# The first norm of a two-block forward pass: rows of x scaled as they land, and a new order of the first weight tile

## The reference

```python
def rms_norm(x, g):
    xf = x.astype(jnp.float32)
    y = xf * lax.rsqrt(jnp.mean(xf * xf, axis=-1, keepdims=True) + NORM_EPS)
    return (y * g.astype(jnp.float32)).astype(x.dtype)

h = rms_norm(x, norm1_g[l])
proj = h @ w_in[l]
...
x = x + (g_a * y_attn + g_b * y_conv) @ w_out[l]
```

## Time and profile before

| | us |
|---|---|
| Median of three executions | 1408.19 (1407.58 to 1408.29) |
| The profiled execution, its own time | 1409.79 |
| Span of the profiled execution | 1407.9 |
| TensorE busy in the span | 1390.3 |
| VectorE, ScalarE, GpSimd busy | 763.4, 599.8, 600.4 |
| Mean granted clock of TensorE | 0.996 |

### The profile page before, as it was taken

The page is one execution under the profiler, slowest core; times in us unless marked ns, Lnnn a source line. Parts: engine busy times, 40 slices in busy tenths (PEclk is TensorE's granted clock), DMA queues, the critical chain, the costliest instruction groups (busy, mean ns, idle before and its releaser), DMA issues.

```text
span 1407.9 us, 20943 instructions
## 1 busy us (share of the span) xinstructions
PE 1390.3 (99%) x7688; PEld 1153.6 (82%) x7688; DVE 763.4 (54%) x1512; ACT 599.8 (43%) x1030; POOL 600.4 (43%) x318
## 2 busy tenths in 40 slices
PE   7999999999999999999999999999999999999998
PEld 6878777778898888888888978878898888888887
DVE  4797865555767665667784848532563232221221
ACT  5322555455345444443222524575354344342222
POOL 8442222115435444444553479623335444444441
PEclk9999999999999999999999999999999999999999
DMA  6941110114524444445763151021213222322321
GB/s 197 204 114 38 60 61 31 31 31 148 181 92 154 150 128 149 134 136 157 219 194 102 61 119 61 31 61 31 90 61 120 89 89 100 109 86 82 108 83 60
DMA packets 187269, 146.15 MB, mean 104 GB/s; under 512 B 21545, under 2 KB 185619, under 8 KB 187200
## 3 DMA queue, kind: packets, MB, share of 16 engines
q1 hardware_dynamic: 185488, 144.59, 34.0%
q10 hardware_dynamic: 1200, 0.36, 0.1%
q0 software_dynamic: 512, 0.25, 0.1%
HBM read 143.08 MB, written 2.10 MB: 103 GB/s over the span
## 4 chain that ended last, share of the span: by engine, by line
PE 87%; DVE 7%; DMA 3%; issue 1%; ACT 1%; SPq 0%; DVEq 0%; ACTq 0%
PE ps L2087 26%; PE ps L2088 25%; PE ps L2089 25%; DMA ada<-in_ada_w 2%; DVE ps L1703 2%; PE ps L2482 2%; PE ps L2234 2%; PE ps L2317 1%; PE ps L2300 1%; DVE ps L1356 1%; DMA raw<-in_w_in 1%; PE ps L2539 1%; PE ps L2509 1%; DVE h_lo L1366 1%; PE ps L2562 1%
## 5 line engine op out<-in xcount | busy, mean ns | idle before, releaser
L789 POOL TENSOR_TENSOR w_lo<-raw,w_hi 128x1024 fp32r<-128x1024 f32 (+2 forms) x224 | 514.7, 2299 | 734.0 <-ACT w_hi L843 453.0
L2087 PE MATMUL ps<-h_hi,w_hi 128*128 128x512 f32 (+1 forms) x1344 | 510.4, 380 | 4.8 <-DVE h_lo L1443 2.5
L2088 PE MATMUL ps<-h_lo,w_hi 128*128 128x512 f32 (+1 forms) x1344 | 498.5, 371 | 0.0
L2089 PE MATMUL ps<-h_hi,w_lo 128*128 128x512 f32 (+1 forms) x1344 | 498.0, 371 | 0.0
L2087 PEld LDWEIGHTS ps<-h_hi,w_hi 128*128 128x128 f32 x1344 | 254.4, 189 | 68.6 <-issue 18.5
L2089 PEld LDWEIGHTS ps<-h_hi,w_lo 128*128 128x128 f32 x1344 | 254.5, 189 | 44.1
L2088 PEld LDWEIGHTS ps<-h_lo,w_hi 128*128 128x128 f32 x1344 | 254.4, 189 | 40.5 <-issue 0.5
L843 ACT ACTIVATE w_hi<-raw 128x1024 fp32r<-128x1024 f32 (+2 forms) x136 | 133.6, 984 | 264.1 <-PE ps L2089 259.9
L1106 ACT ACTIVATE w_hi<-raw 128x1024 fp32r<-128x1024 f32 x88 | 93.1, 1058 | 222.3 <-PE ps L2089 222.3
L2087 PE MATMUL ps<-g_hi,w_hi 128*128 128x512 f32 (+1 forms) x394 | 146.6, 372 | 0.0
L2088 PE MATMUL ps<-g_lo,w_hi 128*128 128x512 f32 (+1 forms) x394 | 144.6, 367 | 0.0
(11 more groups left out here) (356 smaller groups left out, 1697.5 us busy)
## 6 DMA issues: line engine op xcount, KB each, us to landing
ada<-in_ada_w SPq DMA_DIRECT2D x48, 512.0 KB, 3.9
raw<-in_w_in SPq DMA_DIRECT2D x22, 1024.0 KB, 5.2
raw<-in_ffn_w_up SPq DMA_DIRECT2D x22, 1024.0 KB, 5.1
raw<-in_w_up SPq DMA_DIRECT2D x22, 1024.0 KB, 5.0
raw<-in_ffn_w_down SPq DMA_DIRECT2D x8, 896.0 KB, 5.8
raw<-in_w_down SPq DMA_DIRECT2D x8, 896.0 KB, 4.9
raw<-in_w_in SPq DMA_DIRECT2D x16, 256.0 KB, 4.4
raw<-in_w_out SPq DMA_DIRECT2D x4, 1024.0 KB, 5.4
```

Source lines behind the costliest of these rows:

```text
L789: pool.tensor_tensor(w_lo[slot % 4][:, 0:nk, :], part[:, :, slot % 2 * P:(slot % 2 + 1) * P], w_hi[slot % 4][:, 0:nk, :].bitcast(F32), ALU ...
L2087: pe.matmul(out_ap, w, x, start=first, stop=False, **kw)
L2088: pe.matmul(out_ap, w, xl, start=False, stop=False, **kw)
L2089: return pe.matmul(out_ap, wl, x, start=False, stop=last, **kw)
```

## The change

- ScalarE and VectorE take the root and the reciprocal of each row block as it comes, and the rows are multiplied by it in place in `x_in` (VectorE block 0 and the first halves of blocks 2 and 3, ScalarE block 1 and the second halves). The squares of block 2 and of half of block 3 are VectorE's multiply-and-sum.
- TensorE turns the scaled rows, seven groups of each block, into ps1 to ps7 (`X_BANK`); the eighth follows inside tile 0, into the bank of k = 0.
- The high part is one ScalarE instruction from PSUM with the gain as scale. The low part is one VectorE instruction from PSUM (gain times column, minus high part); GpSimd makes none.
- `xT` is the column group times the spread roots (`plain_x`), all eight on VectorE, after the low parts except for k = 0. TensorE spreads the roots instead of the reciprocals, into ps0.
- Dummies: eleven ahead of block 0's turns, two and one further on, in place of 7 and 18.
- Tile 0 is written out: for k = 0 to 2 only hi x hi and hi x lo, then the turns of k = 7, then the rest, with the held-back lo x hi matmuls in between.
- The weights of tiles 0 and 1 come as two transfers of 128 columns each (512 B runs instead of 1 KB), with a semaphore of its own for the first. `hi(1)` stands between the high parts of k = 2 and 3.
- GpSimd's tables move behind `lo(2)`.
- `sc_at`, where the score buffers and `x_in` begin, moves from 210944 to 211072 bytes in the partition.

The core of the diff:

```diff
-        sc_at = offset[0] = aligned(offset[0])
+        sc_at = offset[0] = aligned(offset[0]) // 256 * 256 + 128
...
-                LOADS[n] = standard(w_in, 1304 + (m % 2) * CONV_CH + (m // 2) * 256, n)
+                LOADS[n] = two_columns(w_in, [1304, 1304 + P], n) if n == 0 else standard(w_in, 1304 + (m % 2) * CONV_CH + (m // 2) * 256, n)
...
-            total[n % 2] += 16 * len(LOADS[n])
+            total[n % 2] += 16 * (len(LOADS[n]) if n else 1)
...
+        X_BANK = [1, 2, 3, 4, 5, 6, 7, 1]
+
+        X_ORDER = [0, 7, 5, 6, 3, 4, 1, 2]
+        X_COPIED = {k: 3 + n for n, k in enumerate(X_ORDER)}
+
+        def column(at, t):
+            return stat[:, at.start + t:at.start + t + 1]
...
-            unit(0)
+
+            for (dst, src), loaded in zip(LOADS[0], (raw_first, raw_in[0])):
+                sp.dma_start(dst, src).then_inc(loaded, 16)
...
             for s in range(S_UP + 4):
                 lo(s)
-                if s == 0:
-                    norm_lo(0, [1])
-                if s == 1:
-                    norm_lo(0, [3, 5, 7])
+                if s == 2:
+                    tables()
...
-                act.wait_ge(raw_in[u % 2], RAW_COUNT[u])
+                if s == 0:
+                    act.wait_ge(raw_first, 16)
+                else:
+                    act.wait_ge(raw_in[u % 2], RAW_COUNT[u])
...
-                for k in range(KD):
-                    act.wait_ge(normed, HN_BASE[norm] + k + 1)
-                    act.activation(h_hi[:, k, :], normed_tile(norm, k), ACT.Copy).then_inc(n_hi, 1)
-
             act.dma_start(rows[0:KD, 0, :], a["norm1_g"].rearrange("a (r c) -> (a r) c", c=P)).then_inc(g1_loaded, 16)
             act.wait_ge(consts, 1)
             load_sqrt()
-            for t in range(QT):
+            def row_root(t, **kw):
+                act.activation(column(SUMS1, t), column(SUMS1, t), ACT.Sqrt, scale=1.0 / D, **kw).then_inc(rooted, 1)
+
+            for t in range(2):
                 act.wait_ge(x_loaded[t], 16)
-                unused = (hn[:, :, :], sq[:, :, :], mg[:, 0:2, :], mg[:, 2:4, :])[t]
-                ins = act.activation(unused.rearrange("p a n -> p (a n)"), x_in[:, t, :], ACT.Square,
-                                     accum_out=stat[:, SUMS1.start + t:SUMS1.start + t + 1])
-            link(ins)
-            act.activation(stat[:, SUMS1], stat[:, SUMS1], ACT.Sqrt, scale=1.0 / D, bias=eps_t[:, 0:1]).then_inc(rooted, 1)
+                link(act.activation((hn, sq)[t].rearrange("p a n -> p (a n)"), x_in[:, t, :], ACT.Square,
+                                    accum_out=column(SUMS1, t)))
+                row_root(t, bias=eps_t[:, 0:1])
+            act.wait_ge(inverted, 2)
+            act.activation(x_in[:, 1, :], x_in[:, 1, :], ACT.Copy, scale=column(INVERSE1, 1)).then_inc(x_scaled[1], 1)
+            act.wait_ge(x_squared, 1)
+            row_root(2, bias=eps_t[:, 0:1])
+            act.wait_ge(x_loaded[3], 16)
+            link(act.activation(qT[:, 2, :], x_in[:, 3, ROW_HALF[0]], ACT.Square, accum_out=column(SUMS1, 3)))
+            act.wait_ge(x_squared, 2)
+            row_root(3, bias=stat[:, LAST_SUM])
+            for t in range(2, QT):
+                act.wait_ge(inverted, t + 1)
+                act.activation(x_in[:, t, ROW_HALF[1]], x_in[:, t, ROW_HALF[1]], ACT.Copy,
+                               scale=column(INVERSE1, t)).then_inc(x_scaled[1], 1)
             hi(0)
-            hi(1)
-            norm_hi(0)
+            act.wait_ge(x_copied, 1)
+            for k in range(KD):
+                act.wait_ge(x_turned, k + 1)
+                act.activation(h_hi[:, k, :], ps[X_BANK[k]][:, :], ACT.Copy, scale=g1[:, k:k + 1]).then_inc(x_hi, 1)
+                if k == 2:
+                    hi(1)
             hi(2)
             hi(3)
-            for k in range(4, KD):
-                act.wait_ge(x_turned, k + 1)
-                act.activation(xT[:, k, :], ps[k][:, :], ACT.Copy).then_inc(x_copied[1], 1)
             act.wait_ge(x_turned, KD)
             act.dma_start(wg[:, :, :], k_tiles(w_in, 0, KD, 1280, 24)).then_inc(wg_loaded, 16)
             hi(4)
...
+            def row_inverse(t):
+                dve.wait_ge(rooted, t + 1)
+                dve.reciprocal(column(INVERSE1, t), column(SUMS1, t)).then_inc(inverted, 1)
+
+            def scaled_rows(t, cols):
+                dve.wait_ge(inverted, t + 1)
+                dve.tensor_scalar(x_in[:, t, cols], x_in[:, t, cols], column(INVERSE1, t), None, ALU.mult).then_inc(x_scaled[0], 1)
+
             dve.wait_ge(first_turned, 1)
-            link(dve.tensor_copy(g1[:, :], ps[7][:, 0:KD]))
-            for k in range(4):
-                dve.wait_ge(x_turned, k + 1)
-                dve.tensor_copy(xT[:, k, :], ps[k][:, :]).then_inc(x_copied[0], 1)
-                if k == 1:
-                    dve.wait_ge(rooted, ROOT[0])
-                    dve.reciprocal(stat[:, INVERSE1], stat[:, SUMS1]).then_inc(inverted, 1)
+            dve.tensor_copy(g1[:, :], ps[7][:, 0:KD]).then_inc(x_copied, 1)
+            row_inverse(0)
+            scaled_rows(0, slice(0, D))
+            row_inverse(1)
+            dve.wait_ge(x_loaded[2], 16)
+            dve.tensor_tensor_reduce(out=qT[:, 0:2, :].rearrange("p a n -> p (a n)"), in0=x_in[:, 2, :], in1=x_in[:, 2, :],
+                                     scale=1.0, scalar=0.0, op0=ALU.mult, op1=ALU.add,
+                                     accum_out=column(SUMS1, 2)).then_inc(x_squared, 1)
+
+            dve.wait_ge(x_loaded[3], 16)
+            dve.tensor_tensor_reduce(out=qT[:, 3, :], in0=x_in[:, 3, ROW_HALF[1]], in1=x_in[:, 3, ROW_HALF[1]],
+                                     scale=1.0 / D, scalar=EPS, op0=ALU.mult, op1=ALU.add,
+                                     accum_out=stat[:, LAST_SUM]).then_inc(x_squared, 1)
+            for t in range(2, QT):
+                row_inverse(t)
+                scaled_rows(t, ROW_HALF[0])
             dve.wait_ge(first_turned, 2)
-            link(dve.tensor_copy(rstd[:, :], ps[7][:, :]))
-            for k in range(KD + 2):
-                if k < KD:
-                    dve.wait_ge(x_turned, k + 1)
-                    if k >= 4:
-                        lo_ready(dve, 0, k - 4)
-                    dve.scalar_tensor_tensor(out=normed_tile(0, k), in0=ps[k][:, :], scalar=g1[:, k:k + 1], in1=rstd[:, :],
-                                             op0=ALU.mult, op1=ALU.mult).then_inc(normed, 1)
-                if k >= 2 and k % 2 == 0:
-                    m = k - 2
-                    dve.wait_ge(n_hi, HN_BASE[0] + m + 1)
-                    dve.tensor_tensor(h_lo[:, m, :], normed_tile(0, m), h_hi[:, m, :].bitcast(F32),
-                                      ALU.subtract).then_inc(n_lo[0], 1)
+            dve.tensor_copy(rstd[:, :], ps[0][:, :]).then_inc(x_copied, 1)
+
+            def x_low(k):
+                dve.wait_ge(x_hi, k + 1)
+                dve.scalar_tensor_tensor(out=h_lo[:, k, :], in0=ps[X_BANK[k]][:, :], scalar=g1[:, k:k + 1],
+                                         in1=h_hi[:, k, :].bitcast(F32), op0=ALU.mult, op1=ALU.subtract).then_inc(x_lo, 1)
+
+            def plain_x(k):
+                dve.tensor_tensor(xT[:, k, :], ps[X_BANK[k]][:, :], rstd[:, :], ALU.mult).then_inc(x_copied, 1)
+
+            x_low(0)
+            dve.wait_ge(x_copied, 2)
+            plain_x(0)
+            for k in range(1, KD):
+                x_low(k)
+            for k in X_ORDER[1:]:
+                plain_x(k)
...
-            pe.wait_ge(consts, 1)
-            for t in range(QT):
-                pe.wait_ge(x_loaded[t], 16)
-                for k in range(KD - 2):
-                    ins = pe.transpose(ps[k][:, t * P:(t + 1) * P], x_in[:, t, k * P:(k + 1) * P], ident[:, :])
+            def turn_rows(t, ks):
+                for k in ks:
+                    ins = pe.transpose(ps[X_BANK[k]][:, t * P:(t + 1) * P], x_in[:, t, k * P:(k + 1) * P], ident[:, :])
                     if t == QT - 1:
                         ins.then_inc(x_turned, 1)
-                if t == 1:
-                    pe.wait_ge(g1_loaded, 16)
-                    pe.transpose(ps[7][:, 0:KD], rows[0:KD, 0, :], ident[0:KD, 0:KD]).then_inc(first_turned, 1)
-            keep_warm(6, 7)
-            pe.wait_ge(inverted, 1)
+
+            pe.wait_ge(consts, 1)
+            pe.wait_ge(g1_loaded, 16)
+            pe.transpose(ps[7][:, 0:KD], rows[0:KD, 0, :], ident[0:KD, 0:KD]).then_inc(first_turned, 1)
+            keep_warm(0, 11)
+            pe.wait_ge(x_copied, 1)
+            pe.wait_ge(x_scaled[0], 1)
+            turn_rows(0, range(KD - 1))
+            keep_warm(0, 2)
+            pe.wait_ge(x_scaled[1], 1)
+            turn_rows(1, range(KD - 1))
+            keep_warm(0, 1)
+            pe.wait_ge(x_scaled[0], 2)
+            turn_rows(2, range(4))
+            pe.wait_ge(rooted, QT)
             for t in range(QT):
-                n = INVERSE1.start + t
```

(62 more changed lines are left out.)

43 lines of the change are left out of this document (18 added, 25 removed).

## The result

The changed kernel takes 1401.52 us, the median of five runs (1400.86 to 1402.97). Its ratio to the kernel before is 0.9946, with an interval of 0.9935 to 0.9957. It is faster, by 7.6 us by that ratio and by 6.8 by the medians. The forecast was 1402.4, a gain of 5.75. The profiled execution of after has a span of 1401.1 and a time of 1403.0, so 1.9 us lie around the span, as before.

The account below looks back on a forecast made before the run. TensorE, busy for 99% of the span, was taken as the bound, so the gain had to lie in the first 27 us: 1408.19 less 5.75 for tile 1's earlier start gave 1402.4 us, range 1400.8 to 1405.8.

Parts of the forecast that it names:

- The start, which carries the sum: First 27 us: tile 1's first matmul starts at 21.15 instead of 26.90 us, 5.75 us gained; forecast's chance 0.52.
- The moved buffers, "takes nothing": Score buffers moved by 128 bytes: bounded by -0.5 and +0.5 us from one TensorE wait, taken as nothing.
- Packets: First weights in 512 B packets at 204 GB/s: first half lands at 11.8 us, second at 14.5.
- rival 2: First weights' load: short packets cost nothing, first half there by 11.15, everything 0.65 us earlier, 1401.8 us; chance 0.09.
- Rival 1, the clock: Sparse TensorE stretch, 12.3 to 16.5 us: granted clock falls, nine gaps 0.2 us longer, costing 1.8 us, 1404.2; chance 0.21.
- Rival 3, low parts behind GpSimd: Tile 0: VectorE's new low parts still sit behind GpSimd, only 1.3 us gained, 1406.9 us; chance 0.13.
- Rival 4, tile 1's split as the stop: ScalarE's queue stands in tile 1's weight split until second half lands; if at 24.5, costs 9.1 us, 1411.5; chance 0.05.
- Scaling and sum of 1024 columns: Row blocks of x on VectorE: scaling taken at 0.97 us, multiply-and-sum at 1.38, upper end 2.05 each.
- Tables: GpSimd's 3.3 us of tables go behind tile 2's low weights, covered, with no TensorE wait at tile 3's start.
- The dummies: TensorE's start: eleven dummies of two passes from about 3 us, lasting until 5.5 to 7.9 us, ahead of later needs.

## Where the prediction was right, and the step that failed

The direction and the mechanism were right. The sum was too small: the gain is 7.6 us by the ratio (6.1 to 9.2) against 5.75. The median of 1401.52 lies within the range; the gain by the ratio is just over the 7.4 of its fast end.

- **The start, which carries the sum: right.** Tile 1 at 20.99 against 21.15; k = 2's second matmul at 16.11 against 16.25, the turns done at 16.80 against 17.0. The kernel with the shift taken back, which is the start alone, gains 6.2 us by its ratio (4.2 to 8.2) against 5.75.
- **The moved buffers, "takes nothing": the step that failed.** The bound of 0.5 either way looked at a wait of TensorE. What moved was the pitch of its matmuls, 0.5 us in the traces. By the times the shift is worth 1.7 us (0.4 to 3.0) to 2.0; what makes up the rest is open, and falls of the clock that come or not by chance could do it.
- **What the sum lacked besides.** In the usual execution the weights' first half is there half a microsecond sooner (next point), so that tile 1 starts at 20.58 with the shift taken back; and tile 1 of before starts at 26.90, 27.08 and 27.30 in three profiles, of which the forecast had the earliest. So 5.75, 0.5 for the packets, 0.5 for the pitch and 0.2 for before make 7.0, an estimate from these profiles that leaves out the falls of the clock. The 0.6 us that are left up to 7.6 lie within the interval.
- **Packets: mis-sized.** I took 204 GB/s from one stretch. The packets of after, from 9 to 12 us and then from 46 to 49, where such packets move too:

```profile
DMA packets 1656, 0.84 MB, mean 281 GB/s; under 512 B 144, under 2 KB 1634, under 8 KB 1656
...
DMA packets 1736, 0.89 MB, mean 297 GB/s; under 512 B 29, under 2 KB 1735, under 8 KB 1735
```

At 281 GB/s the half takes 1.85 us, not 2.6, and lands at 11.1; ScalarE, free at 11.1 to 11.3, is the bound. That the profile of after met 11.8 was luck: x itself landed 0.5 us later there (9.23 against 8.72). So rival 2's time for the first split is the usual one, at a rate between the two that I weighed. The 368 GB/s of 1 KB packets still stands above both.
- **Rival 1, the clock: partly true.** It fell in four of the ten profiled starts with the new order, one of them the changed kernel itself, the other three variants of it; priced at 1.8, measured 1.6. The price was met by luck: it was taken from before's nine slow matmuls, and there the fall cost 0.3 to 0.7.
- **Rival 3, low parts behind GpSimd: no.** 0.75 and 0.68 us; from SBUF they do, 2.38.
- **Rival 4, tile 1's split as the stop: no.** The half landed at 13.13 in the run that waits for it, needed by 15.4.
- **Scaling and sum of 1024 columns: 0.75 and 1.21 us**, under the 0.97 and 1.38 taken, far from the upper end of 2.05. Tables: no wait of tile 3, as said. The dummies: right on their length (the 22 passes end at 7.6, with 7.9 the late end), but their worth, which I did not price, is 1.1 us.
- **Two gaps in the compressed score**, 0.46 us between the first two traces, were in no term. Runs put them down to chance.

## What to carry to other kernels

When buffers move in a change, time the move alone: 128 bytes that the forecast took at nothing were worth 0.5 us in the traces and 1.7 (0.4 to 3.0) in the times. Before a count of events is put down to a change, look at what else sorts the same profiles. Price a stall by what is late next, since the same fall of the clock cost 0.3 to 0.7 us where another engine set the pace and 1.6 where TensorE did. And a transfer rate read in one stretch is no bound; look at a second stretch of the same packets, and at whether the engine that wants them is free at all.

## What the hardware showed that I had not expected

- A 128x512 matmul whose streamed activations lie 128 bytes further is issued 0.007 us sooner (0.70 against 0.68 us for three), in all ten profiles with the shift and all four without.
- The same program differs between executions by 1.5 to 1.6 us for each fall of the clock, near 134 to 142 and 966 to 974 us. Executions of before with a mean granted clock of 1.000 take 1406.0 (8 of 69), those with 0.996 take 1409.9 (26). The one of after at 1.000 took 1398.94.
- TensorE was busy throughout when the clock fell near 970 us. The fall follows a group of 24 matmuls of a single column, and comes only in those executions in which a point of the clock's raster lies 2.6 to 3.9 us behind the group's start. Why a busy TensorE loses its clock there no run tests. The group's first eight and last eight in before's timeline of TensorE, and the slow matmuls behind them:

```profile
970.78 0.95 PE L2516 MATMUL ps<-ones,qd 128*128 128x1 f32 x8
...
972.48 1.03 PE L2516 MATMUL ps<-ones,qd 128*128 128x1 f32 x8
973.38 0.54 PE L2087 MATMUL ps<-h_hi,w_hi 128*128 128x512 f32 x1
973.72 0.63 PE L2088 MATMUL ps<-h_lo,w_hi 128*128 128x512 f32 x1
```
